# Norms of a two-layer decoder trunk done token tile by token tile: the last four weight pairs of the output projections reordered, final weights loaded early, score products widened

## The reference, cut to what matters

```python
for layer in range(DEPTH):
    mod = cond @ ada_w[layer] + ada_b[layer]
    sh1, sc1, g1, sh2, sc2, g2 = jnp.split(mod[:, None, :], N_MOD, axis=-1)
    h = rms_norm(x) * (1.0 + sc1) + sh1
    y = even_mixer(h, ...) if layer % 2 == 0 else odd_mixer(h, ...)
    x = x + g1 * y
    h = rms_norm(x) * (1.0 + sc2) + sh2
    x = x + g2 * swiglu(h, ffn_w_in[layer], ffn_w_out[layer])
return rms_norm(x, final_norm)
```

## Time and profile before

| | us |
|---|---|
| median of 3 runs | 2265.13 |
| the 3 runs | 2264.85, 2265.13, 2268.84 |
| the profiled execution's own time | 2264.14 |
| its span, first to last instruction | 2262.3 |
| PE busy in the span | 2162.9 (96%) |
| DVE busy | 1621.3 (72%) |
| ACT busy | 964.8 (43%) |

### The profile page before, as it was taken

One profiled execution on the slowest core, in us unless ns is written; L12 is line 12 of the kernel. 1 busy time (PEld: TensorE's weight loads), 2 busy tenths in 40 slices (PEclk: granted clock), 3 DMA queues, 4 the chain that ended last, 5 costly groups with the idle time before them and its releaser, 6 DMA issues.

```text
span 2262.3 us, 26365 instructions
## 1 busy us (share of the span) xinstructions
PE 2162.9 (96%) x10092; PEld 1797.7 (79%) x10092; DVE 1621.3 (72%) x1683; ACT 964.8 (43%) x1261; POOL 9.9 (0%) x22
## 2 busy tenths in 40 slices
PE   3799999989999999999999999989999999999997
PEld 2578888778888888888887888878888888888885
DVE  5989898897789988777667666586765545455554
ACT  4344444444443344434445444454443344434443
POOL 0000000000000000000000000000000000000000
PEclk9899999999999999999999999999999999999998
DMA  9977877878889999987664533348765555555533
GB/s 391 421 287 312 318 311 303 321 287 357 334 321 369 380 386 376 361 304 288 260 245 190 174 126 117 133 178 312 278 242 187 196 191 188 186 194 197 186 149 149
DMA packets 82447, 594.10 MB, mean 263 GB/s; under 512 B 9296, under 2 KB 9328, under 8 KB 10672
## 3 DMA queue, kind: packets, MB, share of 16 engines
q1 hardware_dynamic: 81072, 588.29, 67.6%
q0 software_dynamic: 1280, 4.51, 0.7%
HBM read 590.66 MB, written 2.10 MB: 262 GB/s over the span
## 4 chain that ended last, share of the span: by engine, by line
PE 47%; issue 36%; DVE 10%; DMA 3%; ACT 2%; DVEq 1%; SPq 0%; POOL 0%; ACTq 0%; POOLq 0%
PE ps L1255 14%; PE ps L1257 14%; PE ps L1256 14%; DVE w_lo L756 3%; DVE ada_raw L760 2%; PE ps L1243 2%; DMA gate<-in_ada 1%; ACT w_hi L460 1%; DMA raw<-in_ab_in 1%; DVE gate L760 1%; DVE spare L760 1%; PE ps L1317 1%; PE ps L1312 1%; PE ps L1315 1%; DVE work L847 0%
## 5 line engine op out<-in xcount | busy, mean ns | idle before, releaser
L756 DVE TENSOR_TENSOR w_lo<-raw,w_hi 128x1024 fp32r<-128x1024 f32 x728 | 880.6, 1223 | 484.7 <-ACT w_hi L460 480.0
L460 ACT ACTIVATE w_hi<-raw 128x1024 fp32r<-128x1024 f32 x728 | 762.1, 1060 | 1005.4 <-PE ps L1257 775.2
L1255 PE MATMUL ps<-w_hi,xT_hi 128*128 128x512 f32 x1952 | 774.0, 396 | 27.9 <-DVE xT_lo L960 23.8
L1257 PE MATMUL ps<-w_hi,xT_lo 128*128 128x512 f32 x1952 | 764.7, 392 | 0.0
L1256 PE MATMUL ps<-w_lo,xT_hi 128*128 128x512 f32 x1952 | 763.7, 391 | 0.0
L1255 PEld LDWEIGHTS ps<-w_hi,xT_hi 128*128 128x128 f32 x1952 | 369.3, 189 | 109.0 <-DVE xT_lo L960 26.1
L1257 PEld LDWEIGHTS ps<-w_hi,xT_lo 128*128 128x128 f32 x1952 | 368.7, 189 | 78.5
L1256 PEld LDWEIGHTS ps<-w_lo,xT_hi 128*128 128x128 f32 x1952 | 369.5, 189 | 74.3
L760 DVE SCALAR_TENSOR_TENSOR ada_raw<-ada_raw,cond 128x2048 f32<-128x2048 f32 x176 | 402.1, 2285 | 19.3 <-DMA ada_raw<-in_ada 18.2
L1255 PE MATMUL ps<-w_hi,hT_hi 128*128 128x512 f32 x960 | 376.9, 393 | 4.0 <-DVE gate L788 1.6
L1257 PE MATMUL ps<-w_hi,hT_lo 128*128 128x512 f32 x960 | 373.9, 389 | 0.0
(11 more groups left out here) (163 smaller groups left out, 832.1 us busy)
## 6 DMA issues: line engine op xcount, KB each, us to landing
ada_raw<-in_ada SPq DMA_DIRECT2D x176, 1024.0 KB, 6.7
raw<-in_ffn_in SPq DMA_DIRECT2D x176, 1024.0 KB, 4.9
raw<-in_ffn_out SPq DMA_DIRECT2D x88, 1024.0 KB, 5.1
raw<-in_ab_in SPq DMA_DIRECT2D x48, 1024.0 KB, 8.8
raw<-in_swa_in SPq DMA_DIRECT2D x20, 1024.0 KB, 4.9
raw<-in_ab_out SPq DMA_DIRECT2D x16, 1024.0 KB, 8.0
raw<-in_swa_out SPq DMA_DIRECT2D x16, 1024.0 KB, 4.8
spare<-in_ada SPq DMA_DIRECT2D x8, 1024.0 KB, 8.2
```

The lines of the kernel that those rows point to most:

```text
L460: nc.scalar.activation(w_hi[:, p % PAIRS, :, :], raw[:, t % RAW, 2 * (p % 2):2 * (p % 2) + 2, :], ACT.Copy).then_inc(hi_ready, 1)
L756: tt(w_lo[:, p % PAIRS, :, :], raw[:, (p // 2) % RAW, 2 * (p % 2):2 * (p % 2) + 2, :], w_hi[:, p % PAIRS, :, :].bitcast(F32), ALU.subtract ...
L1255: mm(out, hi[:, kt, tok], w_hi[:, q % PAIRS, k, :], start=(kt == 2 * ps0), stop=False)
L1257: last = mm(out, lo[:, kt, tok], w_hi[:, q % PAIRS, k, :], start=False, stop=(kt == 2 * ps1 - 1))
```

## The change

Four things are changed.

The last four pairs of the three projections ahead of norms 1, 2 and 3 and of the last one are used in another order (`token_tiles`): first all four pairs for token tile 0 (24 matmuls), which is then announced (`half_used`), then the same four pairs for token tile 1, each pair being given free at its end.

The norms go by token tile. VectorE updates token tile 0's last block, makes its mean square and inverse and its `xn`, then does the same for token tile 1; two of the four blocks of token tile 1's `xn` go to ScalarE. The `hi` and `lo` of the next projection's pairs 0 and 1 move from ahead of the update into the norm. TensorE transposes token tile 0's blocks in the order 0, 2, 3, 1 (block 1 goes into the banks that hold the last accumulation), then those of token tile 1. For the odd mixer, gate times the first half of the last block is added to `x` in the loop after its pair 24 (`last_first_half`).

The final weights are loaded into `spare` early in the second feed-forward layer.

In `scores`, token tile 1's product against the first and the second 128 keys is one matmul of 256 columns, and the masks are added behind it.

```diff
-            pool.wait_ge(evacuated, EVAC_CREDIT + chain[-1].block0 + 4)
-            pool.dma_start(gate[:, :], T["final_norm"].partition_broadcast(P)).then_inc(final_landed, 16)
+            pool.wait_ge(evacuated, EVAC_CREDIT + FFN[1][0][1].block0)
+            pool.dma_start(spare[:, :], T["final_norm"].partition_broadcast(P)).then_inc(final_landed, 16)
...
+            def norm(n, ready, nxt=None):
+
+                act.wait_ge(x_half, n)
+                square_tile(NB - 1, 0).then_inc(ssq_half[0], 1)
+                act.wait_ge(ms_half[0], n)
+                nc.scalar.activation(rstd[:, 2:3], ssq[:, 2:3], ACT.Sqrt).then_inc(root_half[0], 1)
+                if nxt:
+                    hi(nxt, 0, 0)
+                    hi(nxt, 0, 1)
+                act.wait_ge(evacuated, ready)
+                square_tile(NB - 1, 1).then_inc(ssq_half[1], 1)
+                act.wait_ge(ms_half[1], n)
+                nc.scalar.activation(rstd[:, 3:4], ssq[:, 3:4], ACT.Sqrt).then_inc(root_half[1], 1)
+                if n == 4:
+                    return
+                act.wait_ge(rstd_last, n)
+                for c in range(2, 4):
+                    nc.scalar.activation(xn[:, 1, c * NT:(c + 1) * NT], x[:, 1, c * NT:(c + 1) * NT], ACT.Copy,
+                                         scale=rstd[:, 1:2]).then_inc(xn_act, 1)
...
-                hi(nxt, 0, 0)
-                hi(nxt, 0, 1)
-                square(NB - 1, EVAC_CREDIT + ph.block0 + ph.n * ph.evacs, n).then_inc(ssq_done, 1)
-                norm(n)
+                norm(n, EVAC_CREDIT + ph.block0 + ph.n * ph.evacs, nxt)
...
+            def normalise(t, c):
+                nc.vector.tensor_scalar(xn[:, t, c * NT:(c + 1) * NT], x[:, t, c * NT:(c + 1) * NT],
+                                        rstd[:, t:t + 1], None, ALU.mult).then_inc(xn_dve[t], 1)
+
+            def norm(n, used, nxt=None):
+
+                j = slice((NB - 1) * NT, NB * NT)
+                for t in range(TT):
+                    if t:
+                        dve.wait_ge(pair_used, used)
+                    else:
+                        dve.wait_ge(half_used, n)
+                    tt(upd[:, t, :], bank(2 + t), gate[:, j], ALU.mult)
+                    dve.drain()
+                    tt(x[:, t, j], x[:, t, j], upd[:, t, :], ALU.add).then_inc((x_half, evacuated)[t], 1)
+                    if t == 0:
+                        mean_square(n, 0)
+                        inverse(n, 0)
+                        if nxt:
+                            for c in range(4):
+                                normalise(0, c)
+                        else:
+                            final_out(0, 0)
+                if nxt:
+                    lo(nxt, 0, 0)
+                else:
+                    final_out(0, 1)
+                mean_square(n, 1)
+                if nxt:
+                    inverse(n, 1).then_inc(rstd_last, 1)
+                    normalise(1, 0)
+                    normalise(1, 1)
+                    lo(nxt, 0, 1)
+                else:
+                    inverse(n, 1)
+                    final_out(1, 0)
+                    final_out(1, 1)
+
+            def final_out(t, h):
+
+                half = slice(h * (D // 2), (h + 1) * (D // 2))
+                stt(out=xn[:, t, half], in0=x[:, t, half], scalar=rstd[:, t:t + 1], in1=spare[:, half],
+                    op0=ALU.mult, op1=ALU.mult).then_inc(xn_done, 1)
...
-                lo(nxt, 0, 0)
-                lo(nxt, 0, 1)
-                last()
-                norm(n, lambda: with_bias(*mods))
+            def to_norm(n, nxt, used, mods):
+
+                with_bias(*mods)
+                norm(n, used, nxt)
...
+            def last_first_half():
+
+                h, j = half_c[3], slice(3 * NT, 4 * NT)
+                tt(h, h, gate[:, j].unsqueeze(1).broadcast_to([P, TT, NT]), ALU.mult)
+                dve.drain()
+                tt(x[:, :, j], x[:, :, j], h, ALU.add)
...
+                if n == 24:
+                    last_first_half()
+            to_norm(3, FFN[1][0][0], USED_CREDIT + C_OUT.pair(0, 32), (1, 3, 2))
...
+            def token_tiles(ph, i, b, slot, hi, lo, q0, p0, first=False):
+
+                for t in range(TT):
+                    out, tok = bank(2 * slot + t), slice(t * P, (t + 1) * P)
+                    for n in range(4):
+                        if t == 0:
+                            pe.wait_ge(lo_ready, LO_CREDIT + ph.pair(i, q0 + n) + 1)
+                        for k in range(2):
+                            kt = 2 * (p0 + n) + k
+                            w = (q0 + n) % PAIRS
+                            mm(out, hi[:, kt, tok], w_hi[:, w, k, :], start=first and n == k == 0, stop=False)
+                            mm(out, hi[:, kt, tok], w_lo[:, w, k, :], start=False, stop=False)
+                            last = mm(out, lo[:, kt, tok], w_hi[:, w, k, :], start=False, stop=n == 3 and k == 1)
+                        if t:
+                            last.then_inc(pair_used, 1)
+                    if t == 0:
+                        last.then_inc(half_used, 1)
...
+                for t, c in ((0, 0), (0, 2), (0, 3), (0, 1), (1, 0), (1, 1), (1, 2), (1, 3)):
+                    if (t, c) == (0, 1):
+                        pe.wait_ge(evacuated, EVAC_CREDIT + ph.block0 + ph.n * ph.evacs)
+                    if t == 0:
+                        pe.wait_ge(xn_dve[0], 4 * (n - 1) + c + 1)
+                    elif c < 2:
+                        pe.wait_ge(xn_dve[1], 2 * (n - 1) + c + 1)
+                    else:
+                        pe.wait_ge(xn_act, 2 * (n - 1) + c - 1)
+                    for kt in range(4 * c, 4 * c + 4):
+                        last = tr(ps[:, kt * SEQ + t * P:kt * SEQ + (t + 1) * P], xn[:, t, kt * P:(kt + 1) * P])
+                    if t:
+                        last.then_inc(xT_done, 1)
...
+                    mm(ps[:, s1:s1 + SEQ], q(h)[:, P:SEQ], k(h)[:, 0:SEQ], start=True, stop=False)
                     if prev_mask:
-                        mm(ps[:, s1:s1 + P], ident_b[:, :], mask_prev[:, :], start=True, stop=False)
-                    mm(ps[:, s1:s1 + P], q(h)[:, P:SEQ], k(h)[:, 0:P], start=not prev_mask, stop=True)
-                    mm(ps[:, s1 + P:s1 + SEQ], ident_b[:, :], mask_own[:, :], start=True, stop=False)
-                    last = mm(ps[:, s1 + P:s1 + SEQ], q(h)[:, P:SEQ], k(h)[:, P:SEQ], start=False, stop=True)
+                        mm(ps[:, s1:s1 + P], ident_b[:, :], mask_prev[:, :], start=False, stop=False)
+                    last = mm(ps[:, s1 + P:s1 + SEQ], ident_b[:, :], mask_own[:, :], start=False, stop=True)
```

More of the change, by code:

```diff
@@ L743, in _ @@
             root_table()
-            square(NB - 1, EVAC_CREDIT + chain[-1].block0 + 4, 4).then_inc(ssq_done, 1)
-            norm(4)
+            norm(4, EVAC_CREDIT + chain[-1].block0 + 4)
         @block.vector
@@ L1226, in _ @@
                     both_halves((n - 22) // 4)
-            to_norm(3, FFN[1][0][0], lambda: both_halves(3), (1, 3, 2))
+                if n == 24:
+                    last_first_half()
+            to_norm(3, FFN[1][0][0], USED_CREDIT + C_OUT.pair(0, 32), (1, 3, 2))
             ffn(1)
-            update(NB - 1, 1, USED_CREDIT + 2 * (chain[-1].quad0 + chain[-1].n * chain[-1].quads), last=True)
-            norm(4)
             dve.wait_ge(final_landed, 16)
-            for n in range(4):
-                t, half = n // 2, slice(n % 2 * (D // 2), (n % 2 + 1) * (D // 2))
-                stt(out=xn[:, t, half], in0=x[:, t, half], scalar=rstd[:, t:t + 1], in1=gate[:, half],
-                    op0=ALU.mult, op1=ALU.mult).then_inc(xn_done, 1)
+            norm(4, USED_CREDIT + 2 * (chain[-1].quad0 + chain[-1].n * chain[-1].quads))
         @block.tensor
@@ L1420, in _, with blocks @@
                     pe.wait_ge(gate_copied, 1)
-            norm_blocks(1, range(4))
-            def blocks(ph, hi, lo, slot=0, x_at=None, before=None, behind=None):
+            token_tiles(AB_OUT, 0, 3, 1, hT_hi, hT_lo, 28, 4)
+            norm_blocks(1, AB_OUT)
+            def blocks(ph, hi, lo, slot=0, x_at=None, before=None, behind=None, tiles=False):
                 def body(i, first=False):
@@ L1428, in body @@
                         pe.wait_ge(evacuated, ph.block(i, b) + 1)
-                        for p in range(ph.pairs):
+                        by_tile = tiles and not first and b == ph.blocks - 1
+                        for p in range(ph.pairs - 4 * by_tile):
                             if first and b == 0 and x_at is not None and p % 2 == 0:
@@ L1437, in body @@
                                 behind(i, b, p, first)
+                        if by_tile:
+                            token_tiles(ph, i, b, (slot + b) % 2, hi, lo, (b + 1) * ph.pairs - 4, ph.pairs - 4)
                 body(0, True)
@@ L1468, in ffn @@
                     blocks(fin, xT_hi, xT_lo, x_at=n_norm if s == 0 else None, behind=behind_in)
```

(2 more changed lines are left out.)

115 lines of the change are left out of this document (49 added, 66 removed).

## The result

The changed kernel took 2250.55 us (median of 4 runs, 2248.42 to 2253.35) beside 2264.99 us of the kernel before (4 runs, 2263.52 to 2268.84): a ratio of 0.9935 with an interval of 0.9919 to 0.9951. That is 14.4 us less. The profiled execution of the changed kernel is the slowest of its four (2253.35).

A forecast was written before the change was run, and what follows sets the result against it. TensorE's work was taken to fill almost the whole span, leaving gains in the norms and the end. Terms 4.5 - 6.6 + 6.7 + 0.8 = 5.4 gave 2258.7 us, plus 1.0 for the median 2259.7; range 2253 to 2263.5.

The forecast's parts named there:

- norms, chains of the three: Inner norms: a shorter chain from last to next first matmul, saving 3.0, 2.4 and 3.3 us at norms 1, 2, 3.
- late split, norms 1 and 3: Last pair's split comes late for token tile 0's earlier matmuls, costing 3.0 us at norm 1 and 1.2 at norm 3.
- half clock, three norms: TensorE's pauses bring half clock around the next projection's first matmuls in all three norms: 2.2 us lost each, 6.6 together.
- the end: Program's end: token tile 0's work done earlier and final weights loaded in time, saving 6.7 us.
- scores: Attention scores: four matmuls at 0.45 us become one wide product at 0.43, saving 0.02 x 48 heads = 0.8 us.
- TensorE does not wait behind them: Next projection's first matmuls: with no TensorE wait following, time lost there to half clock counts, 1.5 to 2.9 us each.
- Rival (a): Inner norms: the clock holds or falls where it does no harm; gain 12.0 us, time 2253.1, chance 0.13.
- The rule that the prediction weighed: Inner norms: if transposes never engage full clock, both kernels start projections at half clock, the 6.6 us loss vanishes, gain 12.0.
- R: VectorE's start of the last update before a norm; forecast: first matmul 9.3 us later, last products at the end 6.1 later.
- the forecast's last step: End of the inner norms' chain: 0.07 us from the first `xT_lo` to the next projection's first matmul.
- (b): Norm 1's last four pairs: clock falls during waits for splits, 2.7 us more lost; gain 2.7, time 2262.4, chance 0.16.
- (c): Behind each inner norm: half clock lasts longer, up to 11.5 us; loss 17.3 instead of 6.6, time 2270.4, chance 0.07.

The follow-up runs named there:

- e3: The changed kernel with scores and end of the kernel before, so only the three inner norms are new: 2264.33 us, ratio 0.9994 to the kernel before.
- e11: The changed kernel's scores with two products of 128 columns instead of one of 256, masks still behind both: 2252.59 us in one run.
- e4: The changed kernel with both TensorE pauses in each inner norm filled by repeated transposes (12 and 20): 2248.96 us, ratio 0.9934 to the kernel before.
- e2: The changed kernel with the end of the kernel before (both token tiles together, final weights loaded late): 2259.16 us, ratio 0.9974 to the kernel before.
- e6: The changed kernel with only the first pause in each inner norm filled, by 12 repeated transposes: 2251.68 us in one run.
- e7: The changed kernel with only the second pause in each inner norm filled, by 20 repeated transposes: 2250.13 us, ratio 0.9933 to the kernel before.
- e10: The changed kernel with two modulation steps ahead of norm 1 done on 64 of 2048 columns (output differs): 2251.32 us in one run.
- e9: The changed kernel with VectorE's last three modulation steps ahead of norm 1 moved behind the last split: 2255.34 us in one run.
- e5: The changed kernel as it is, run again beside the versions with repeated transposes: 2250.88 us, ratio 0.9935 to the kernel before.

## Why the prediction was wrong

Term by term, in us gained:

| term | forecast | found |
|---|---|---|
| norms, chains of the three | 8.7 | 9.6 |
| late split, norms 1 and 3 | -4.2 | -4.2 (PE's waits for `w_lo`) |
| half clock, three norms | -6.6 | -2.7 on average over twelve steps, 0 to -4.5 |
| the end | 6.7 | 7.1 |
| scores | 0.8 | 5.0 |
| sum | 5.4 | 14.8, measured 14.4 (11.1 to 18.3 by the interval) |

The first three lines add up to 2.7, and e3 measured 1.4 for them (-0.7 to 3.4). With the 1.8 found below for the half clock they add up to 3.6 and the sum is 15.7. That the sum comes so near the measured time is in part luck.

**The step that failed is the price of the scores.** "A head has nine matmuls in 1.01 us, 0.112 each" spread the time evenly over unlike instructions: a mask takes half of that, a pass of a product 0.11 or 0.14 according to what stands ahead of it (e11). So the four passes priced at 0.45 took 2 x 0.28 = 0.56, each product behind a mask, and the wide one takes 0.44, behind none: 0.12 a head, and 0.06 where the previous mask is missing and only one product stood behind a mask. That is 32 x 0.125 + 16 x 0.06 = 5.0. The single rows stood in the trace of before, as shown under the result. The upper bound of the term, 5.4, held; but the range was not stretched to it, and the result lies 2.5 us below its low end.

**The second is a size, the half clock.** The mechanism was right: it comes in the pauses, and where it falls on the first matmuls it costs. "In all three norms" was not. In the nine profiles with the new norms and no repeats it fell on the first matmuls in 16 norms of 27 and on the last 16 transposes in the other 11 (3.2 to 3.6 us for them in place of 1.97), in a mixture from norm to norm; over the twelve steps the loss was 1.2 to 2.4 where it fell there, 1.5 on average, under the 2.2 taken. The profiled execution of the changed kernel lost 4.1, more than most. That is part of why the two profiles differ by only 10.7; another 1.9 us is lost ahead of the first scores (161.78 us into the span, 159.93 before), in code that the change leaves alone.

That "TensorE does not wait behind them" did not hold either. At norms 1 and 3 the kernel before waits for VectorE's split ahead of the 49th matmul, and the changed kernel, late by its half clock, does not (norm 1, before and changed):

```profile
496.79 0.47 PE L1255 MATMUL ps<-w_hi,xT_hi 128*128 128x512 f32 x1 [0.60 <-DVE w_lo L756]
```

```profile
498.49 0.39 PE L1308 MATMUL ps<-w_hi,xT_hi 128*128 128x512 f32 x1
```

Against e4, where the clock held, the changed kernel has lost 1.5, 1.6 and 1.4 us at the 48th matmul behind the three norms, and 0.6, 1.6 and 0.5 at the 201st. So 0.9 of a loss at norms 1 and 3 comes back, and over the nine profiles 1.8 us a run are left of 2.8 at the 48th. From norm 3's first matmul to the program's last one it is 731.22 to 731.27 us in e2, e3, e4, e6, e7 and e10, where that norm lost nothing, and 731.65 to 731.99 in the six profiles where it lost 1.2 to 1.6 over the twelve steps.

Rival (a), that the clock holds, is not what happened, and the gain went beyond its time for another reason.

The rule that the prediction weighed (the Trainium skill, TensorE: Matmul & The Clock Gate, Part 4: PE-mode transpose, that the full clock does not engage for transposes) speaks against the repeats of e4 and e7: they should have changed nothing. The traces disagree: without them half clock on the first matmuls in 16 norms of 27, with the second pause filled by transposes alone in none of 9, though in one of them it stood on the transposes.

**Right, or nearly:** from R to the first matmul 9.0 for 9.3, though the forecast's last step was misread: the rows of norm 2 have 1228.63 - 1228.13 = 0.50 from `xT_lo` to the matmul, not 0.07. There the transposes last until 1222.32 + 6.56 = 1228.88, at a granted clock of 0.50 from 1223 to 1228, so the half clock seems not to have been quite free before either; in the changed kernel the step takes 0.10 (1228.62 behind 1227.29 + 1.23).

```profile
1222.32 6.56 PE L1243 MATMUL ps<-ident,work 128*128 128x128 f32 x32 [5.46 <-DVE work L806]
```

Right as they stood: the waits inside norm 1's last four pairs; the last products 5.9 behind R for 6.1, with no wait for the weights. The two moved splits and `last_first_half` left no wait of their own. Rivals (b) and (c) did not come: in the changed kernel's profile the clock is 1.00 from 462 to 477 us, over norm 1's last pairs and their waits, and the longest loss behind a norm in any profile was 2.4 us over the twelve steps, 2.8 over 24. Norm 1's split had the size forecast, but as a bound it was half the story: e9 and e10 show VectorE and the modulation loads behind it at nearly the same time.

## What to carry to other kernels

Price removed instructions from their own rows, with the one ahead of each, and never from the mean of a mixed series; and let the range reach the bound that the text itself has worked out. Before a wait is counted as a gain, look for what would be late next: at norm 1 both ways of removing 3 us of waiting gave half a microsecond or a loss. Where a short pause ahead of a long run of matmuls costs the clock, repeated transposes with the same result can keep it: here they kept the half clock off the matmuls in 9 of 9 norms, at 0.46 us in one of them and nothing in the others. That they shorten the run was not shown: neither e4 nor e7 is faster than the changed kernel beyond the noise.

## What was not expected of the hardware

A bfloat16 mask of 128 columns between f32 products costs 0.055 us itself and 0.055 more in the product behind it (0.28 against 0.22 for two passes, e11). So gathering the masks saves what merging the products was thought to. And the place of the half clock is not the program's alone: in e5 the same code met it on the matmuls at norm 1 and 3 and on the transposes at norm 2.
